# Picking each expert's token rows with a 0/1 matrix on TensorE instead of sorting them through DRAM

## The reference, cut to what matters

```python
h = layer_norm(ALPHA * x + merged @ lw['w_out'], ...)
pg_top, g_idx = lax.top_k(softmax(h @ w_rg + b_rg), 1)        # one group of 4
pe_top, e_idx = lax.top_k(softmax(le_sel), 2)                  # two of its 8 experts
gates = pg_top * pe_top / sum(pe_top)
# rows of one expert, in blocks:
hid = silu(xi @ w_gate[e]) * (xi @ w_up[e])
y += (hid @ w_down[e]) * gate
ple = sigmoid(h @ ple_w_gate) * (p @ ple_w_proj)
x_new = layer_norm(ALPHA * h + moe + ple, ln2_g, ln2_b)
```

## Time and profile before

| | |
|---|---|
| Median of 3 runs | 1675.69 us (1672.64 to 1677.7) |
| The profiled execution, its own time | 1676.81 us |
| Its span, first to last instruction | 1675.2 us |
| PE busy in the span | 1488.9 us (89%) |
| DVE, ACT, POOL busy | 579.7, 159.5, 256.2 us |
| Bytes moved by DMA | 520.12 MB, mean 310 GB/s |

### The profile page before, as it was taken

One profiled execution on the slowest core, in us unless ns is written; L12 is line 12 of the kernel. 1 busy time (PEld: TensorE's weight loads), 2 busy tenths in 40 slices (PEclk: granted clock), 3 DMA queues, 4 the chain that ended last, 5 costly groups with the idle time before them and its releaser, 6 DMA issues.

```text
span 1675.2 us, 23013 instructions
## 1 busy us (share of the span) xinstructions
PE 1488.9 (89%) x8909; PEld 962.3 (57%) x8909; DVE 579.7 (35%) x1053; ACT 159.5 (10%) x336; POOL 256.2 (15%) x371
## 2 busy tenths in 40 slices
PE   8899999999999789998798898897988988879786
PEld 6677676767777646655454455354544544546443
DVE  6989999994110541111111112111111111112115
ACT  3122222223000300000000000000000000000001
POOL 3658777720000010000000000000000000000001
PEclk7999999999999789999999999999999989999998
DMA  7546453533596199999999999999999999999995
GB/s 184 141 124 155 114 156 97 159 114 92 155 297 228 49 335 405 410 404 411 415 402 415 417 412 409 408 418 411 400 405 410 398 417 400 415 417 404 407 405 202
DMA packets 175992, 520.12 MB, mean 310 GB/s; under 512 B 23680, under 2 KB 135440, under 8 KB 148400
## 3 DMA queue, kind: packets, MB, share of 16 engines
q1 hardware_dynamic: 160752, 486.12, 75.6%
q10 hardware_dynamic: 12832, 16.85, 3.1%
q0 software_dynamic: 2304, 15.74, 3.0%
HBM read 496.32 MB, written 22.36 MB: 310 GB/s over the span
## 4 chain that ended last, share of the span: by engine, by line
DMA 43%; PE 33%; DVE 15%; issue 6%; SPq 2%; ACT 1%; POOL 0%; DVEq 0%; ACTq 0%; POOLq 0%
DMA e_ring<-in_w_exp_up_dram 32%; PE bank L1530 11%; DMA e_ring<-in_w_exp_gate_dram 10%; PE bank L1136 8%; PE bank L1555 4%; PE bank L1461 3%; DVE e_ring L1781 3%; PE bank L1380 2%; DVE e_ring L1774 2%; DVE e_ring L1785 2%; PE bank L1310 2%; SPq L613 1%; DVE e_ring L1777 1%; DVE e_ring L1790 1%; DVE e_ring L1789 1%
## 5 line engine op out<-in xcount | busy, mean ns | idle before, releaser
L1530 PE MATMUL bank<-e_ring,xT_exp 128*64 128x256 f32 x4096 | 480.8, 393 | 94.9 <-DMA e_ring<-in_w_exp_gate_dram 54.9
L1530 PEld LDWEIGHTS bank<-e_ring,xT_exp 128*64 128x64 f32 x4096 | 299.2, 142 | 285.3 <-DMA e_ring<-in_w_exp_gate_dram 71.8
L1555 PE MATMUL bank<-e_ring,hidT 128*64 128x512 f32 x1024 | 239.5, 622 | 36.4 <-DVE hidT L2154 36.4
L1136 PE MATMUL bank<-xT,w_ring 128*128 128x288 f32 x1024 | 269.0, 418 | 0.7 <-issue 0.7
L1136 PEld LDWEIGHTS bank<-xT,w_ring 128*128 128x128 f32 x1024 | 193.9, 194 | 61.4 <-issue 11.0
L2147 DVE TENSOR_TENSOR hid<-bank,sig_exp 128x256 f32<-128x256 f32 x32 | 13.6, 424 | 560.8 <-ACT sig_exp L1074 539.8
L1555 PEld LDWEIGHTS bank<-e_ring,hidT 128*64 128x64 f32 x1024 | 73.6, 142 | 179.8 <-issue 135.1
L813 POOL DMA_INDIRECT e_ring<-expert_rows_out,idx x4 | 3.8, 956 | 1044.1 <-ACT all_stored_mark L828 1043.2
L1461 PE MATMUL bank<-hT,w_ring 128*128 128x288 f32 (+2 forms) x640 | 137.3, 374 | 0.0
L1461 PEld LDWEIGHTS bank<-hT,w_ring 128*128 128x128 f32 x640 | 111.8, 193 | 20.2 <-issue 0.8
L2166 DVE COPY rows<-bank 128x512 f32<-128x512 f32 x31 | 21.4, 691 | 226.4 <-PE bank L1555 226.4
(11 more groups left out here) (381 smaller groups left out, 1220.3 us busy)
## 6 DMA issues: line engine op xcount, KB each, us to landing
e_ring<-in_w_exp_gate_dram SPq DMA_DIRECT2D x64, 2048.0 KB, 27.2
e_ring<-in_w_exp_up_dram SPq DMA_DIRECT2D x63, 2048.0 KB, 28.1
e_ring<-in_w_exp_down_dram SPq DMA_DIRECT2D x63, 2048.0 KB, 21.9
w_ring<-in_w_in_dram SPq DMA_DIRECT2D x32, 1024.0 KB, 6.4
w_ring<-in_w_out_dram SPq DMA_DIRECT2D x16, 1024.0 KB, 6.0
w_ring<-in_w_ple_gate_dram SPq DMA_DIRECT2D x16, 1024.0 KB, 23.8
expert_rows_out<-hT POOLq DMA_DIRECT2D x3, 1536.0 KB, 10.4
w_ring<-in_ssm_w_glu_dram SPq DMA_DIRECT2D x4, 1024.0 KB, 5.2
```

Source lines behind the costliest of these rows:

```text
L1136: last_mm = pe.matmul(out, weights(k), moving[:, k, :], start=(k == 0), stop=(k == n - 1))
L1530: mm = pe.matmul(gu[h * B:(h + 1) * B, s % 2, :], xT_exp[:, c, s // 2, :], w[:, c, h * FH:(h + 1) * FH], start=(s == 0 and c == 0), stop=( ...
L1555: mm = pe.matmul(bank[h * B:(h + 1) * B, y_bank + n, :], hidT[:, c, half, :], e_ring[:, 2 * (NGU + half) + c, h * DH2 + n * 512:h * DH2 + ...
```

## The change

- `x_pick` is done for every expert. Its matrix `x_sel` (tokens by 64 slots) is built by DVE in a new function `select`: four instructions that compare each token's two row numbers, less the expert's first row, with the slot numbers 0 to 63. For this the small table of first rows, `tab_f`, is computed on all 128 partitions instead of one.
- `x_pick(b + 2)` stands on PE behind `down(b)`; ACT copies its result from PSUM to `x_exp` (new `x_copy` on ACT), and `x_turn` reads it as before.
- Gone are the DRAM buffer `rows_by_expert`, one store of padding, the six scatters of POOL, and ACT's row loads with their table reads and branches.
- `rows` must now stay intact, so `x_exp` and `y_exp` move to slot 2 of `w_ring`, which held the gain of LayerNorm 2; that gain (1 MB, broadcast) is now loaded behind the last expert's weights into `hT`.
- The first expert has an order of its own: DVE applies gain and bias in two halves, so that `gate_up(0)` can begin on the first; the small product and transposes of `last_sel_turn` stand ahead of `gate_up(0)`; one PLE chunk and `x_turn(1)` stand inside `hid_turn(0)`. SyncE's load of the second PLE gate slice moves behind the four gate and up pieces of expert 1.

```diff
-        xs_dram = nc.dram_tensor("rows_by_expert", (XROWS, D), F32, kind="Internal").ap()
-        x_exp = rows[:, 0, 0:DH2]
-        y_exp = rows[:, 1, 0:DH2]
+        x_exp = w_ring[:, 2, 0:DH2]
+        y_exp = w_ring[:, 2, DH2:D]
...
# SyncE
+            sp.wait_ge(ple_done, PLE_BLOCKS)
+            sp.dma_start(ln2_gain, ln2_g[0].partition_broadcast(P)).then_inc(gb2_landed, 16)
...
# POOL
-            for k in range(2):
-                for t, (_, m) in enumerate(TT):
-                    pool.indirect_dma_start(xs_dram[:, :], bass.IndirectOffsetOnAxis(ap=idx[0:m, k, t:t + 1], axis=0),
-                                            rows[0:m, t, :], None).then_inc(rows_sorted, 16)
...
# ACT
-            def x_load(b, further=False, turned=None):
...
+            def x_copy(b):
+                act.wait_ge(x_picked, b + 1)
+                copy(x_exp, bank[:, 1:3, :].rearrange("p b n -> p (b n)")).then_inc(x_exp_ready, 1)
...
# PE
+            def x_pick(b, first=False):
+                pe.wait_ge(x_sel_ready, b + 1)
...
                 for n in range(2):
                     for t, (_, m) in enumerate(TT):
                         for h in range(2):
+                            mm = pe.matmul(bank[h * B:(h + 1) * B, 1 + n, :], x_sel[0:m, t, :],
                                            rows[0:m, t, h * DH2 + n * 512:h * DH2 + (n + 1) * 512], start=(t == 0), stop=(t == NT - 1))
...
             def expert(b, middle=None, ahead=True):
                 gate_up(b)
                 x_turn(b + 1)
                 if middle is not None:
                     middle()
                 hid_turn(b)
                 pe.wait_ge(ye_act, b)
                 pe.wait_ge(ye_dve, b)
                 down(b, 3)
+                if ahead:
+                    x_pick(b + 2)
...
+            def first_expert():
+                gate_up(0, first=True)
+                x_pick(1)
+                hid_turn(0, first_hidden)
+                pe.wait_ge(last_sel_copied, 2)
+                down(0, 3)
+                x_pick(2)
...
+            x_pick(0, True)
+            first_gate((3,), slice(0, 1))
+            x_turn(0)
+            first_gate((3,), slice(1, 2))
+            last_sel_turn()
+            first_expert()
...
# DVE
+            def select(b):
+                dve.tensor_tensor(x_slot, sums[:, 0:2, :], tab_f[:, ds(b, 1)].unsqueeze(1).to_broadcast([P, 2, NT]), ALU.subtract).then_inc(x_slot_ready, 1)
+                dve.wait_ge(x_slot_ready, b)
+                slots = io_rows[:].unsqueeze(1).to_broadcast([P, NT, B])
+                at1, at2 = (x_slot[:, k, :].unsqueeze(2).to_broadcast([P, NT, B]) for k in range(2))
+                dve.wait_ge(x_picked, b)
+                dve.tensor_tensor(x_sel2, slots, at2, ALU.is_equal)
+                dve.tensor_tensor(x_sel[:], slots, at1, ALU.is_equal).then_inc(x_hit_ready, 1)
+                dve.wait_ge(x_hit_ready, b)
+                dve.tensor_tensor(x_sel[:], x_sel[:], x_sel2, ALU.add).then_inc(x_sel_ready, 1)
```

More of the change, by code:

```diff
@@ L1109, in _ @@
             count = further_blocks(act, lambda i: expert(i + NM, False, further=True))
-            expert(count + NM, False)
+            expert(count + NM, ahead=False)
             act.wait_ge(ew_used, count * NEW + (NL * NEW + NGU))
@@ L1450, in _, with ple_gate @@
                 route_back(t)
-            def ple_gate(n, j, slot, landed, early=False, chunks=(0, 1, 3, 2)):
+            def ple_gate(n, j, slot, landed, early=False, chunks=(0, 1, 3, 2), parts=slice(None)):
                 pe.wait_ge(w_landed[slot], landed)
@@ L1458, in ple_gate @@
                 for c in chunks:
-                    for out, t0, t1, opens in ple_part(c):
+                    for out, t0, t1, opens in ple_part(c)[parts]:
                         for k in range(4):
@@ L1514, in x_turn, with gate_up @@
                 mm.then_inc(xeT_ready, 1)
-            def gate_up(b, in_halves=False, between={}):
-                pe.wait_ge(xeT_copied, b + 1)
+            def gate_up(b, in_halves=False, between={}, first=False):
+                pe.wait_ge(xeT_copied, 1 if first else b + 2)
                 gu = bank[:, 0, :].rearrange("p (g n) -> p g n", g=2)
                 for s in range(NGU):
+                    if first and s == 2:
+                        pe.wait_ge(xeT_copied, 2)
                     if s in between:
@@ L1558, in down, with expert @@
                     mm.then_inc(ew_used, 1)
-            def expert(b, first, middle=None):
+            def expert(b, middle=None, ahead=True):
                 gate_up(b)
@@ L1566, in expert, with first_gate, first_hidden @@
                 hid_turn(b)
[L1567 to L1571, removed]
-                down(b, 3)
+                pe.wait_ge(ye_act, b)
+                pe.wait_ge(ye_dve, b)
+                down(b, 3)
+                if ahead:
+                    x_pick(b + 2)
+            def first_gate(chunks, parts=slice(None)):
+                ple_gate(0, 0, 0, 16 * (NCH + 2 + KC // 4), True, chunks, parts)
+            def first_hidden():
+                first_gate((2,))
+                x_turn(1)
+            def first_expert():
[5 more added lines that the diff above has]
+                x_pick(2)
             def last_sel_turn():
@@ L1598, in _ @@
                     pair(n, j)
-            expert(PLE_END, False)
-            count = further_blocks(pe, lambda i: expert(i + NM, False))
-            expert(count + NM, False)
+            expert(PLE_END)
+            count = further_blocks(pe, lambda i: expert(i + NM))
+            expert(count + NM, ahead=False)
             def tile_banks(t):
@@ L2154, in hidden_copy, with expert @@
                 dve.tensor_copy(hidT[:].rearrange("p c h n -> p (c h n)"), bank[:, 0, 0:FC * B]).then_inc(hidT_copied, 1)
-            def expert(b, first, middle=None):
+            def expert(b, middle=None, ahead=True):
+                if ahead:
+                    select(b + 2)
                 hidden(b)
@@ L2163, in expert @@
                 dve.wait_ge(ew_used, b * NEW + NEW)
-                if not first:
-                    dve.wait_ge(ye_stored, b * 32)
+                dve.wait_ge(ye_stored, b * 32)
                 dve.tensor_copy(y_exp[:, 512:DH2], bank[:, 4, :]).then_inc(ye_dve, 1)
@@ L2199, in _ @@
                     pair(n, j)
-            expert(PLE_END, False)
-            count = further_blocks(dve, lambda i: expert(i + NM, False))
-            expert(count + NM, False)
+            expert(PLE_END)
+            count = further_blocks(dve, lambda i: expert(i + NM))
+            expert(count + NM, ahead=False)
             b = count + NL
```

175 lines of the change are left out of this document (83 added, 92 removed).

## The result

Measured: 1733.7 us in the median of 4 runs (1731.2 to 1737.99), against 1674.53 us for the kernel before in its runs beside it. The ratio is 1.0354 (95% interval 1.0324 to 1.0384): slower by 59 us. The prediction said 1711, range 1695 to 1728. Its direction and its mechanism hold; the size missed by 23 us and the range by 6.

What follows compares the result with a forecast made beforehand. DMA was taken to bound the expert loop, PE nearly full; the change hands the bound to PE. PE's serial times with picks add 26 us, the clock 10: 1675.7 + 36 gives 1711.7, stated as 1711, range 1695 to 1728.

Steps and rivals of the forecast that it cites:

- The bound changed hands: In the expert loop, per eight experts, PE needs 271.8 us and DMA 262.5, so PE sets the time instead of DMA.
- The pick at 5.74 us, unhidden: Each added `x_pick`, between `down(b)` and `gate_up(b+1)` on PE, costs 5.74 us with nothing hiding it.
- Eight experts at 271.8 us plus some clock: PE's time per loop block: 225.8 us plus 45.9 for picks; 10 us in all added for clock loss.
- The clock behind the stall: At `down` behind eleven 2.22 us PE stalls, lowered clock adds 10 us; ends 0 and 32.
- Rival 3: At experts without a PLE part, the clock falls at every stall, or DVE's stall grows: 1720 to 1734 us; chance 0.14.
- the end of `gate_up(31)`: Last expert on PE: `gate_up(31)` takes 13.9 us and about 5 for the twenty transposes between its pieces.
- The row loads at 5.2 us per eight experts: On ACT's queue in the loop, removing row loads takes 5.2 us per eight experts off DMA's 267.7.
- the room for a pick: PE time free per expert in the loop before DMA stops being the limit: 4.6 us.
- Rival 1: In the expert loop, DMA still sets the end and the kernel gets faster: 1655 us; chance 0.06.
- `select`, ACT's copies, the late gain at nothing: DVE's `select` and ACT's pick copies are covered during `gate_up`; the late gain load costs 0 to 3 us, taken as 0.
- The first expert: At the start, a 6.02 us wait goes and two picks, 11.5 us, come; `gate_up(1)` starts 0.7 us earlier.
- rival 2: At PE's stalls, the clock stays full, since falls may have echoed long waits: 1702 us; chance 0.10.

Runs made afterwards that it cites:

- e4: Kernel before, with twelve matmuls of the pick's form added at the end of experts 0 to 30, result unused, row loads kept: 1745.73 us.
- e2: Changed kernel, with PE's loop over the three blocks of eight experts written out: 1719.82 us.
- e6: Changed kernel, with two 128 by 512 matmuls put into the 2.2 us stall of experts without a PLE part: 1715.35 us.
- e5: Changed kernel, picks of experts 1 to 31 with the first token tile alone, 4 matmuls: 1620.13 us.
- e9: Kernel before, each row load cut to one row per half, same number of loads: 1624.65 us.
- e10: Kernel before, each row load with all 64 rows per half, same number of loads: 1743.78 us.
- e3: Changed kernel, picks of experts 1 to 31 without the third token tile, 8 matmuls instead of 12: 1656.11 us.

## Why the prediction missed

**The bound changed hands: right.** No wait for weights is left, DMA's 43% of the chain is 0. e4 shows it from the other side: the picks alone, with the row loads kept, lose all of it.

**The pick at 5.74 us, unhidden: right.** It is 5.69 in the flow, 5.73 by the length of an expert. An expert with a gate part was summed at 36.71 and took 36.70.

**Eight experts at 271.8 us plus some clock: the step that failed.** The blocks took 1051.52 - 771.05 = 280.5 us and 1329.16 - 1051.52 = 277.6. Two terms of the sum were mis-sized.

- *The branch, not in the sum at all: 13.1 us.* I took PE's serial time from experts 1 to 4 and from inside a block, none of which has a branch behind it. The kernel before has the same three branches. Two were covered there by waits for weights (the 1.87 and 2.61 above), so the trace put their idle time down to DMA; the third stood in the rows that I showed, as "issue 2.9", and I passed over it. e2 gives 14 us for it.
- *The clock behind the stall: 16.0 us, not 10.* I carried over the loss of before as if it were a property of the stall. Nine of eleven stalls lost time now, five before. e6 shows that it is a clock matter and what it is worth, 17.6 us with the last expert's `down`. Rival 3 (all fall, 19 us) was nearer. That the measured time also lies in its 1720 to 1734 is luck: the falls make up 6 of the missing 23 us, and the branches, which it doesn't have, more than half.

The rest is small: the end of `gate_up(31)` 0.8 and the tail 1.6 us more than summed (the tail is one more fall of the clock, which e6 took away), the part up to expert 1 3.4 less, of which 2.8 lie ahead of the first pick, where the change does next to nothing and which varies by some us between the runs. 13.1 + 6.0 + 0.8 + 1.6 - 3.4 = 18, and the profiled span is 54.3 us up where 36 were summed. The other 4 us are no part of the mechanism: the median is 2.5 above the profiled execution, where before it was 1.1 below.

**The row loads at 5.2 us per eight experts: wrong, without effect on the forecast.** They took about 14 (267.7 - 254; e5, e9, e10). I priced them by their queue's share of packet time; what they cost is what the other queue no longer moves. At 417 GB/s the weights of eight experts (316.39 MB in 800 us is 105.9 MB in 267.7) need 254 us, not 262.5, so the room for a pick was (254 - 225.8) / 8 = 3.5 us and not 4.6. Rival 1's floor, 1655, is 1620 to 1625 for the same reason. The direction wasn't touched, since 5.74 is more than either; a pick of 4 us would have been misjudged. e3's 3.43 us is just within.

**`select`, ACT's copies, the late gain at nothing: right**, by e4, to a few us. **The first expert: right.** From the first pick to `gate_up(1)` it takes 628.35 - 582.52 = 45.83 us where it was 632.47 - 585.28 = 47.19: a gain of 1.4, with 0.7 forecast.

**Falls as an echo of long waits (rival 2): wrong.** The falls grew in number as the waits went, from five to nine.

## What to carry to other kernels

When an edit moves a kernel from one bound to another, sum the new bound's engine from end to end, edges included: an idle time that the trace puts down to the old bound may have a second reason under it, and it comes out when the first goes. Look for a row that names "issue" at the same kind of place. Price a transfer by what the queue beside it moves with and without it, not by its own share. And once an engine is the bound, its smallest stalls are worth more than they look: three DVE instructions in another order were worth 37 us on one side of the change of bound and nothing on the other.

## What the runs showed of the hardware that I had not expected

- Row loads of 4 KB rows from DRAM cost 7 to 7.7 us of DMA time per MB beside a weight stream at 2.4 us per MB, while their queue's share of packet time says 2.95.
- At a stall of 2.2 us the granted clock went from 1.00 to 0.50 late in the stall or early in the matmuls behind it, in nine cases of eleven, at 1.4 to 3.0 us each.
- Matmuls that compute nothing, 1.9 us of them in a 2.2 us stall, made the kernel 15 to 18 us faster, with the granted clock at 0.984 in place of 0.972.
- Four 32-row matmuls of the pick in four parts of the array, and not two: 1.1 us less per pick, from 5.69 to 4.55.
- The heads of the second and third block of a loop cost PE 4.0 and 4.2 us (idle time and slow first matmuls). Writing out the loop took this away, and the 5.0 us ahead of a later branch as well.
